# Three mixer products between token unit halves, and statistics ahead of the norm at both expert stage ends

## What is computed

```python
def reference(x, positions, ...):
    h = x
    for layer in range(DEPTH):
        mix = _mixer_ab(h, ...) if layer % 2 == 0 else _mixer_cd(h, ...)
        h = _layernorm(DEEPNORM_ALPHA * h + mix, ln_mix_g[layer], ln_mix_b[layer])
        ffn = _moe(h, w_router, b_router, moe_w_gate[layer], moe_w_up[layer], moe_w_down[layer])
        h = _layernorm(DEEPNORM_ALPHA * h + ffn, ln_ffn_g[layer], ln_ffn_b[layer])
    return h

def _mixer_ab(x, ...):
    rq, rk, rv, rg, mq, mk, mv, mo, mi, mf = _split(x @ w_in, RET_SPLITS + ML_SPLITS)
    y_ret = _head_norm(_retention(q, k, v), RET_H, ret_norm_g, True) * jax.nn.silu(rg)
    h = _mlstm(q, k, v, i_pre, logf) * jax.nn.sigmoid(mo)
    return concat([y_ret, _head_norm(h, ML_H, ml_norm_g, True)]) @ w_out

def _mixer_cd(x, ...):
    gq, gk, gv, gr, ga, sz, sxbc, sdt = _split(x @ w_in, GLA_SPLITS + SSD_SPLITS)
    y_gla = _head_norm(_gla(q, k, v, log_alpha), GLA_H, gla_norm_g, False) * jax.nn.silu(gr)
    ...                                     # SSD branch
    return concat([y_gla, y_ssd]) @ w_out
```

## Time and profile before

| | us |
|---|---|
| median of 3 runs | 1004.25 |
| lowest and highest run | 999.66 and 1004.96 |
| the profiled execution | 1006.0 |
| its span, first to last instruction | 1004.2 |

### The profile page before, as it was taken

The page is one execution under the profiler, slowest core; times in us unless marked ns, Lnnn a source line. Parts: engine busy times, 40 slices in busy tenths (PEclk is TensorE's granted clock), DMA queues, the critical chain, the costliest instruction groups (busy, mean ns, idle before and its releaser), DMA issues.

```text
span 1004.2 us, 10005 instructions
## 1 busy us (share of the span) xinstructions
PE 964.2 (96%) x3984; PEld 514.2 (51%) x3984; DVE 298.6 (30%) x773; ACT 223.9 (22%) x466; POOL 15.3 (2%) x29
## 2 busy tenths in 40 slices
PE   8989999999999999989999999999999999999986
PEld 7644775554543355333385557888445433443322
DVE  4230162321431212120335433564316111131203
ACT  1120243211121112110202433431532121111101
POOL 2000000000000000000000000000000000000001
PEclk9999999999999999999999989999999999999999
DMA  8982334153789999999994423352655899999993
GB/s 275 333 317 88 134 118 149 61 210 125 270 342 404 422 422 412 397 420 421 396 388 157 156 85 118 134 210 79 241 224 211 324 399 421 420 422 420 419 418 148
DMA packets 65780, 278.86 MB, mean 278 GB/s; under 512 B 8852, under 2 KB 9216, under 8 KB 41920
## 3 DMA queue, kind: packets, MB, share of 16 engines
q1 hardware_dynamic: 63856, 271.60, 69.0%
q0 software_dynamic: 1872, 6.53, 1.9%
HBM read 277.04 MB, written 1.06 MB: 277 GB/s over the span
## 4 chain that ended last, share of the span: by engine, by line
PE 79%; DMA 15%; DVE 3%; issue 1%; ACT 1%; SPq 0%; DVEq 0%
PE bank L698 75%; DMA ring<-in_moe_w_up 14%; PE bank L1068 1%; DMA ring<-in_w_in_ab 1%; PE bank L1429 1%; PE bank L1073 1%; PE bank L794 1%; PE bank L975 0%; ACT feat L1497 0%; PE bank L1016 0%; DVE stat L2279 0%; ACT rstd L1497 0%; DVE hT L2286 0%; DVE h L2521 0%; DVE yT L2389 0%
## 5 line engine op out<-in xcount | busy, mean ns | idle before, releaser
L698 PE MATMUL bank<-ring,hT 128*64 128x512 f32 (+1 forms) x800 | 277.1, 604 | 11.6 <-DMA ring<-in_moe_w_up 5.4
L698 PE MATMUL bank<-ring,feat 128*64 128x512 f32 (+1 forms) x1152 | 228.5, 595 | 2.9 <-ACT feat L1497 2.7
L698 PEld LDWEIGHTS bank<-ring,hT 128*64 128x64 f32 (+1 forms) x800 | 108.5, 165 | 161.0 <-issue 153.3
L698 PE MATMUL bank<-hT,ring 128*128 128x256 f32 x768 | 168.4, 380 | 1.3 <-DMA ring<-in_w_in_ab 1.1
L698 PEld LDWEIGHTS bank<-hT,ring 128*128 128x128 f32 x768 | 145.8, 191 | 21.4 <-DMA ring<-in_w_in_ab 1.9
L1497 ACT ACTIVATE feat<-bank 32x512 f32<-32x512 f32 (+3 forms) x128 | 60.9, 494 | 388.2 <-PE bank L698 244.6
L698 PEld LDWEIGHTS bank<-ring,feat 128*64 128x64 f32 (+1 forms) x1152 | 74.1, 131 | 142.5 <-issue 131.1
L698 PE MATMUL bank<-ring,yT 128*128 128x512 f32 x256 | 112.8, 595 | 0.0
L2269 DVE COPY feat<-bank 32x512 f32<-32x512 f32 (+1 forms) x56 | 38.5, 687 | 145.7 <-PE bank L698 145.2
L698 PEld LDWEIGHTS bank<-ring,yT 128*128 128x128 f32 x256 | 47.8, 190 | 55.5 <-issue 54.6
L2259 DVE TENSOR_TENSOR feat<-feat,bank 128x512 f32<-128x512 f32 x16 | 11.0, 688 | 175.8 <-PE bank L698 175.8
(11 more groups left out here) (251 smaller groups left out, 568.7 us busy)
## 6 DMA issues: line engine op xcount, KB each, us to landing
ring<-in_moe_w_up SPq DMA_DIRECT2D x60, 1024.0 KB, 17.1
ring<-in_moe_w_gate SPq DMA_DIRECT2D x56, 1024.0 KB, 14.2
ring<-in_moe_w_down SPq DMA_DIRECT2D x56, 1024.0 KB, 12.1
ring<-in_w_in_ab SPq DMA_DIRECT2D x24, 1024.0 KB, 9.1
ring<-in_w_in_cd SPq DMA_DIRECT2D x24, 1024.0 KB, 13.5
ring<-in_w_out_ab SPq DMA_DIRECT2D x8, 1024.0 KB, 5.9
ring<-in_moe_w_down SPq DMA_DIRECT2D x16, 512.0 KB, 17.3
ring<-in_w_out_cd SPq DMA_DIRECT2D x8, 1024.0 KB, 6.0
```

What stands on the lines that cost most here:

```text
L698: return nc.tensor.matmul(o, l, r, start=start, stop=stop)
```

## The change

Five places. `fix` gets bank 5 of its own, and the flips of all later pair jobs so fall the other way: `ab4` goes to banks 0 and 1, `ab5` to 2 and 3, and so on down to `cd11`. On PE, `ab4`'s first half comes ahead of `fix`, `ab11`'s first half comes between `s_ml(2)` and `s_ml(3)`, and `y_gla(2)` with four of the eight products of `cd5`'s second half come ahead of `s_gla(3)`. On DVE, at both expert stage ends, the statistics of bank 7 and the second moments are taken ahead of the norm of the first tokens.

```diff
@@ plan
-        single_job("fix")
+        job("fix", 5)
@@ PE, layer 0
             gate_turns()
+            token_unit("ab4", unit_no(0, 4), (0,))
             b0 = first_of("fix")
             claim("fix", b0)
             pe.wait_ge(fix_in, 1)
             mm(bank[b0][:, 0:4 * EXPERTS], all_ones, route[:, 4:6, :, :].rearrange("p a t e -> p (a t e)")) \
                 .then_inc(ready[b0], 1)
-            for u in (4, 5):
-                token_unit(f"ab{u}", unit_no(0, u))
+            token_unit("ab4", unit_no(0, 4), (1,))
+            token_unit("ab5", unit_no(0, 5))
@@ PE, layer 0
             s_ml(2)
+            token_unit("ab11", unit_no(0, 11), (0,))
             s_ml(3)
-            token_unit("ab11", unit_no(0, 11))
+            token_unit("ab11", unit_no(0, 11), (1,))
@@ PE, layer 1
             token_unit("cd5", unit_no(1, 5), (0,))
+            y_gla(2)
+            token_unit("cd5", unit_no(1, 5), (1,), range(KC // 2))
             s_gla(3)
-            y_gla(2)
-            token_unit("cd5", unit_no(1, 5), (1,))
+            token_unit("cd5", unit_no(1, 5), (1,), range(KC // 2, KC))
             y_gla(3)
@@ DVE, end of layer 0
             def unit_norm(t):
-                shifted(t)
                 b = 4 + 2 * t
 ...
             moe(0)
-            unit_norm(0)
+            shifted(0)
             ffn_stats(0, 1, (1,))
             moments(1)
+            unit_norm(0)
+            shifted(1)
             unit_norm(1)
@@ DVE, end of layer 1
-            last_norm(0)
+            shifted(0)
             ffn_stats(1, 1, (1,))
             moments(1)
+            last_norm(0)
+            wait_root()
             last_norm(1)
```

More of the change, by code:

```diff
@@ L2517, in last_norm @@
             def last_norm(t):
-                shifted(t) if t == 0 else wait_root()
                 for q in range(t + 1):
```

## The result

The changed kernel took 990.92 us in the median of 4 runs (990.35 to 991.75), the kernel before 1002.93 (4 runs, 999.66 to 1004.96; the three of before and one more). The medians lie 12.0 us apart. The ratio on record, which is not the quotient of the two medians, is 0.9871 with a 95% interval of 0.9853 to 0.9890: 12.9 us less, between 11 and 15. The forecast was 991.3, with a range of 986.5 to 996. The profiled execution took 991.75 us with a span of 989.8.

The account below looks back on a forecast made before the run. PE was taken as the bound, busy 96% of the span, so gains come from its waits and the low clock behind two. 5.7 + 1.9 + 5.7 - 0.3 + 0 = 13.0 us, giving a median of 991.3, range 986.5 to 996.

Parts of the forecast that it names:

- The four waits: PE waits in the mixers: 1.43 and 1.10 us round `fix`, 1.86 at `s_ml(3)`, 2.25 at `s_gla(3)`.
- the rival at 998.9 or 1004.6: Expert stages: the weight stream takes the gain back, in layer 0 (998.9, 4%) or both layers (1004.6, 2%).
- Place 1: At `fix`, `ab4`'s first half goes ahead: saves 5.7 us, 2.53 of waits and 3.19 of low clock; at least 2.5.
- Place 2: At `s_ml(3)`, half of `ab11` goes ahead and removes the 1.86 us wait: saves 1.9 us.
- left the clock alone: Behind the 1.86 us wait at `s_ml(3)` every window read 1.00, so no low clock was counted there.
- Place 3: At `s_gla(3)`, `y_gla(2)` and four `cd5` products go ahead: saves 5.7 us, 2.25 of wait and 3.48 of low clock.
- The cushions: Round `s_gla(3)`: 1.7 us to spare for `p_gla(2)` before `y_gla(2)`, 2.3 for the scaled keys; if they fail, nothing saved.
- Flipped banks: Pair jobs after `fix`: each unit still opens the banks of the unit before last, so zero effect.
- Place 4: End of layer 0's experts: DVE gains 0.6 us, but first transposes start later and filling products delay `cd0`; loss of 0.3.
- Place 5: End of layer 1's experts: a 0.64 us earlier last norm, lost because L2526 must wait for POOL's L685; gain 0.
- The step to the median: Profiled execution, 1006.0 us, becomes 993.0; it was 1.75 above the median, and the same distance gives 991.3.
- The rival of one low stretch (994.5): The low clock stays or moves: one stretch at half clock costs 3.2 us, giving 994.5; chance 10%.

Follow-up runs that it names:

- place 3 alone: The kernel before with only `y_gla(2)` and half of `cd5`'s second half put ahead of `s_gla(3)`: 998.88 us, ratio 0.9947 (0.9930 to 0.9964).
- twelve runs: The kernel before with only `ab11`'s first half put between `s_ml(2)` and `s_ml(3)`, measured a second time: 1001.36 us, ratio 0.9972 (0.9955 to 0.9989).
- the repeat: The changed kernel measured again with no edit, against the kernel before: 990.59 us in 6 runs, ratio 0.9889 (0.9870 to 0.9908).

## Why the prediction was right, point by point

- **What bounds it.** Right. The four waits, with the low clock round them, were the gain, and each of the three mixer parts that was put in alone reached the end. The stream took nothing back: the last expert products of layer 0 start 8.7 us earlier and those of layer 1 14.2, so the rival at 998.9 or 1004.6 is out.
- **Place 1**, 5.7 forecast, 5.8 in the profile. The split was 2.5 and 3.2; the stretches give 2.7 for the waits and up to 3.1 for the clock. Wrong in it: that the low clock is the waits' doing alone. It came in two of seven profiles with the waits gone, and once ahead of waits that were there. The changed kernel's own profile had none, which was luck in part.
- **Place 2**, 1.9 forecast, 2.1 in the profile; I took the bracket of 1.86 for the wait, where from start to start it is more. The step "left the clock alone" did not hold in general: the wait did so in five of six profiles that have it, and did not in that of place 3 alone. So the place is worth 2.1 and, over many executions, probably more: 2.8 (1.1 to 4.5) in twelve runs, 4.5 (2.7 to 6.2) in six.
- **Place 3**, 5.7 forecast, 5.8 in the profile. The cushions held: `p_gla(2)` ended at 582.17, 1.75 us ahead of `y_gla(2)`, where 1.7 was forecast. But the 3.5 us of clock in it are the long case of three, and the profiles of other executions show 0 and 1.7 as well.
- **Flipped banks**, zero, and zero.
- **Place 4**, a loss of 0.3 forecast, 0.0 measured. The mechanism is the one described: the first transposes came 5.67 us behind the start of the last expert products, as forecast, and the filling products then held the second ones back; taking them out gave 0.48. The term that was off is the filling: I took 1.0 and 1.5 us, the lengths of merged rows, where from start to start they take 0.87 and 1.30.
- **Place 5**, 0 forecast, 0.2 gained. The lock between L2529 and L685 is shown by the run with POOL's work cut. The size was a bit off: I had the last norm follow L685's end by 0.67 us, and it followed by 0.48. The rule of the Trainium skill ("SBUF — State Buffer", "Who interferes with whom") that I had weighed said 0, without it 0.64; measured 0.2, and 0.7 with POOL out of the way. So the trace agrees that the two exclude each other, but not that the second waits for the whole of the first: L2529 began 0.67 us before L685's end and took only 0.47 longer than alone.
- **The sum and the median.** 13.0 forecast; 14.4 of span in the profiles, of which 13.9 in the stretches of the change; 12.9 and 11.1 by the ratios. The step to the median was lucky in its kind: my profile of before had the long low clock at both places, which is at the dear end of what the profiles of the untouched places show, and I took its distance of 1.75 to the median as a mere offset. A part of that distance was probably clock that other executions did not lose. The rival of one low stretch (994.5) did not come in the median. Single executions of the changed kernel may still have one: in the repeat the one whose clock reads 0.994 took 992.15 us; the slowest, 993.58, reads 0.996.

No version was faster than the changed kernel by more than the scatter. Taking the first filling products out saves 0.5 us in the trace and nothing that the time shows.

## What to carry to other kernels

A wait of TensorE of about 2 us can be followed by low clock that costs another 1.7 or 3.3 us, and whether it is changes from one execution to the next: read several profiles before a part of a sum is called certain, and price the wait and the clock apart. Filling such a wait with products that nobody reads can save at most the clock (1.7 us here at all three places together); putting real work there saves both. And before a step is taken ahead of a wait, look for filling work that was put there to bridge it, and read distances from start to start.

## What the runs showed of the hardware that was not expected

- The clock went down to 0.50 behind waits of 1.86 us in one of six profiles, of 2.25 us in six of seven, and of 1.80 us ahead of L1316 in none of seven. At `fix` it went down in two of seven profiles with no wait at all, behind about 2 us of products that use four rows of the array, and in one more at 70.4, where those products end and the wait begins. A short low stretch in a mixer cost 1.7 us, a long one 3.3 or 3.4 at `s_gla(3)` and 2.0 to 3.1 at `fix`, where a part of it can lie in PE's own waits. A short one in layer 0's expert stage left no loss that the scatter of that stage shows.
- Products of 128x128 by 128x256 that filled a wait of 2.25 us had a clock of 1.00 behind them in the one profile that had them; with the wait left empty that was so in one of seven.
- POOL's and DVE's instructions with two SBUF inputs hold each other up: 1.22 and 1.59 us instead of 0.75 and 1.26, for the one that starts second.
